# A decoder layer whose second feed-forward stage runs in two passes, with seven block products in place of eight

## The reference, cut to what matters

```python
def layer_norm(x, g, b):
    mu = jnp.mean(x, -1, keepdims=True)
    var = jnp.mean(jnp.square(x - mu), -1, keepdims=True)
    return (x - mu) * lax.rsqrt(var + LN_EPS) * g + b

def swiglu(h, wg, wu, wd):
    return (jax.nn.silu(h @ wg) * (h @ wu)) @ wd

# x: 1024 prompt tokens and 8 sample tokens, D_MODEL = 1024; D_FF = 2816
h = x * (1 + mod[:, 1]) + mod[:, 0]
x = layer_norm(ALPHA * x + 0.5 * mod[:, 2] * swiglu(h, ffn1_wg, ffn1_wu, ffn1_wd), ln_g[0], ln_b[0])
h = x * (1 + mod[:, 4]) + mod[:, 3]
x = layer_norm(ALPHA * x + mod[:, 5] * mixer(h), ln_g[1], ln_b[1])      # ends with mixed @ w_out
h = x * (1 + mod[:, 7]) + mod[:, 6]
x = layer_norm(ALPHA * x + 0.5 * mod[:, 8] * swiglu(h, ffn2_wg, ffn2_wu, ffn2_wd), ln_g[2], ln_b[2])
```

## Time and profile before

| | |
|---|---|
| Runs | 2271.41, 2273.47, 2273.75 us, median 2273.47 |
| Span of the profiled execution, first to last instruction | 2265.1 us (8.4 below the median of the runs; no device time of its own is listed) |
| Mean granted TensorE clock | 0.986 |
| Busy share of the span: TensorE, VectorE, ScalarE, GpSimd | 95%, 34%, 26%, 27% |
| TensorE's share of the chain that ended last | 87% |
| First matmul of the second feed-forward stage | 1459.97 us |
| Last down matmul of it, end | 2220.2 us |
| Mean DMA rate | 76 GB/s |

### The profile page before, as it was taken

The page is one execution under the profiler, slowest core; times in us unless marked ns, Lnnn a source line. Parts: engine busy times, 40 slices in busy tenths (PEclk is TensorE's granted clock), DMA queues, the critical chain, the costliest instruction groups (busy, mean ns, idle before and its releaser), DMA issues.

```text
span 2265.1 us, 33136 instructions
## 1 busy us (share of the span) xinstructions
PE 2161.6 (95%) x13244; PEld 1976.8 (87%) x13244; DVE 778.9 (34%) x1709; ACT 580.7 (26%) x1071; POOL 614.4 (27%) x397
## 2 busy tenths in 40 slices
PE   6799999999999998999979989999999999999997
PEld 2689999999999997998844449899999999999995
DVE  1532122321223229202365652751222211222327
ACT  2311111112111123422265561361111111111114
POOL 1232322223222230124233333132323232323210
PEclk8899999999999999999989999999999999999999
DMA  8372222321321110413242012111111111111002
GB/s 288 131 231 94 84 66 93 112 93 38 112 93 38 47 38 19 148 47 108 101 169 106 1 38 66 38 47 48 56 37 56 37 56 37 56 37 56 28 1 75
DMA packets 168942, 171.36 MB, mean 76 GB/s; under 512 B 14370, under 2 KB 130834, under 8 KB 168324
## 3 DMA queue, kind: packets, MB, share of 16 engines
...
## 4 chain that ended last, share of the span: by engine, by line
PE 87%; DVE 6%; ACT 2%; issue 2%; SPq 2%; DMA 1%; POOL 0%; DVEq 0%; ACTq 0%
PE psum L211 26%; PE psum L213 25%; PE psum L212 25%; PE psum L1086 2%; PE psum L546 2%; PE psum L1145 1%; PE psum L987 1%; DVE NT L694 1%; PE psum L1443 1%; DMA ADA<-in_w_ada 1%; SPq L499 1%; PE psum L644 1%; DVE Y L659 1%; DVE Y L679 1%; PE psum L1136 1%
## 5 line engine op out<-in xcount | busy, mean ns | idle before, releaser
L211 PE MATMUL psum<-Hhi,Whi 128*128 128x344 f32 x2736 | 878.7, 321 | 19.5 <-DVE Hlo L703 10.3
L213 PE MATMUL psum<-Hhi,Wlo 128*128 128x344 f32 x2736 | 875.2, 320 | 0.0
L212 PE MATMUL psum<-Hlo,Whi 128*128 128x344 f32 x2736 | 874.4, 320 | 0.0
L313 POOL TENSOR_TENSOR Wlo<-RAW,Whi 128x1024 fp32r<-128x1024 f32 x158 | 383.2, 2446 | 696.9 <-ACT Whi L309 696.3
L211 PEld LDWEIGHTS psum<-Hhi,Whi 128*128 128x128 f32 x2736 | 515.9, 189 | 29.9 <-issue 23.0
L213 PEld LDWEIGHTS psum<-Hhi,Wlo 128*128 128x128 f32 x2736 | 515.6, 188 | 0.0
L212 PEld LDWEIGHTS psum<-Hlo,Whi 128*128 128x128 f32 x2736 | 514.9, 188 | 0.3
L436 DVE TENSOR_TENSOR GF<-SIL,psum 128x344 f32<-128x344 f32 x132 | 67.6, 512 | 902.7 <-ACT SIL L400 900.1
L443 DVE SCALAR_TENSOR_TENSOR Y<-psum,G,Y 128x344 f32<-128x344 f32 (+1 forms) x528 | 301.2, 573 | 180.5 <-PE psum L213 180.5
L211 PE MATMUL psum<-Ghi,Whi 128*128 128x344 f32 x1056 | 340.2, 322 | 2.4 <-DVE Y L443 2.4
L212 PE MATMUL psum<-Glo,Whi 128*128 128x344 f32 x1056 | 338.0, 320 | 0.0
(11 more groups left out here) (192 smaller groups left out, 1312.0 us busy)
## 6 DMA issues: line engine op xcount, KB each, us to landing
...
RAW<-in_ffn_wg SPq DMA_DIRECT2D x44, 512.0 KB, 3.8
RAW<-in_ffn_wu SPq DMA_DIRECT2D x44, 512.0 KB, 3.7
RAW<-in_ffn_wd SPq DMA_DIRECT2D x44, 512.0 KB, 3.7
...
```

The costliest lines, as they stand in the source:

```text
L211: pe.matmul(out, whi, xhi, start=first, stop=False)
L212: pe.matmul(out, whi, xlo, start=False, stop=False)
L213: return pe.matmul(out, wlo, xhi, start=False, stop=last)
L313: pool.tensor_tensor(Wlo[slot][:, :, :], RAW[raw][:, :, :], Whi[slot][:, :, :].bitcast(F32), ALU.subtract).then_inc(W[phase].ready, 1)
```

## The change

The second feed-forward stage handles the tokens in two passes of 516, each as two sides of `GQ = 258`. In a pass, a chunk takes two tiles of `D_FF` (rows j), two halves of `D_MODEL` (LOWK, HIGHK) and the two sides: a product of 2 by 2 blocks, for the gate and for the up weights. Its eight block products become seven of sums and differences of blocks (`NP = 7`), so 14 products for gate and up, each of 12 matmuls with 258 columns. VectorE forms the sums of weight blocks anew for each chunk and pass (`row_sums`, `row_differences`, 512 elements each), and those of the activations once per pass (`column_sums`, `last_column_sum`). Parts of results shared by several blocks are copied from PSUM by ScalarE (`part_act`) and added by VectorE (`add_dve`). A chunk in a pass then has 16 down units of six matmuls with 258 columns; the down weights are the old ones. All weights are fetched and split once per pass, so twice.

The second norm, the w_out product and the third norm go by four groups of 258. The norm of groups 2 and 3 before the stage runs inside the first pass; the last norm of groups 1 and 0 and the output of their first four blocks of 128 tokens run inside the second pass (`early_turn_pe`, `early_copy_act`, `early_sp`); five blocks are left for after the end. The residual scaling of `Y` goes to GpSimd for groups 0 and 1 (`residual_pool`) and ScalarE for 2 and 3 (`residual_act`).

The core of the diff:

```diff
+GQ = T // 4
+NP = 7
...
+        LOWK, HIGHK = slice(0, KT // 2), slice(KT // 2, KT)
+        W_SOURCE = [[PAIR[u][:, 0, LOWK, :], PAIR[u][:, 0, HIGHK, :], S2[u][:, :, :], S1[u][:, :, :],
+                     PAIR[u][:, 1, LOWK, :], PAIR[u][:, 0, HIGHK, :], PAIR[u][:, 1, HIGHK, :]] for u in range(2)]
...
+        T_SOURCE = [NQ[0][:, LOWK, :], NQ[0][:, HIGHK, :], TS[1][:, :, :], TS[0][:, :, :],
+                    NQ[1][:, LOWK, :], NQ[1][:, HIGHK, :], TS[0][:, :, :]]
...
+        BLOCKS = ((0, 0), (1, 1), (0, 1), (1, 0))
...
+        def pair_fetch(sp, r, f, u, first=False):
+            if not first:
+                sp.wait_ge(r_ready, PR * r + u - 1)
+            for j in range(2):
+                sp.dma_start(PAIR[u][:, j, :, :], pair_source[u][:, :, bass.ds((f + j) * P, P)]).then_inc(pair_in[u], 16)
...
+        def row_sums(dve, r, first=False):
+            for u in range(2):
+                if u == 0 and not first:
+                    dve.wait_ge(r_ready, PR * r - 6)
+                dve.wait_ge(pair_in[u], 32 * r + 32)
+                dve.tensor_tensor(S1[u][:, :, :], PAIR[u][:, 1, LOWK, :], PAIR[u][:, 1, HIGHK, :], ALU.add).then_inc(sums_done, 1)
+            for u in range(2):
+                dve.wait_ge(sums_done, 8 * r + 1 + u)
+                dve.tensor_tensor(S2[u][:, :, :], S1[u][:, :, :], PAIR[u][:, 0, LOWK, :], ALU.subtract).then_inc(sums_done, 1)
+        def row_differences(dve, r):
+            for u in range(2):
+                a21 = PAIR[u][:, 1, LOWK, :]
+                dve.tensor_tensor(a21, PAIR[u][:, 0, LOWK, :], a21, ALU.subtract).then_inc(sums_done, 1)
+            for u in range(2):
+                a12 = PAIR[u][:, 0, HIGHK, :]
+                dve.wait_ge(r_ready, PR * r + 3 + u)
+                dve.wait_ge(sums_done, 8 * r + 3 + u)
+                dve.tensor_tensor(a12, a12, S2[u][:, :, :], ALU.subtract).then_inc(sums_done, 1)
...
+        def column_sums(dve, p):
+            dve.wait_ge(t_src, NP * p + 3)
+            if p:
+                dve.wait_ge(t_ready, NP)
+            dve.tensor_tensor(TS[0][:, :, :], NQ[1][:, LOWK, :], NQ[0][:, LOWK, :], ALU.subtract).then_inc(t_src, 1)
+            dve.wait_ge(t_src, NP * p + 4)
+            dve.tensor_tensor(TS[1][:, :, :], NQ[1][:, HIGHK, :], TS[0][:, :, :], ALU.subtract).then_inc(t_src, 1)
+            b12 = NQ[1][:, LOWK, :]
+            dve.tensor_tensor(b12, NQ[1][:, HIGHK, :], b12, ALU.subtract).then_inc(t_src, 1)
+        def last_column_sum(dve, p):
+            dve.wait_ge(t_ready, NP * p + 4)
+            dve.wait_ge(t_src, NP * p + 5)
+            dve.tensor_tensor(TS[0][:, :, :], NQ[0][:, HIGHK, :], TS[1][:, :, :], ALU.subtract).then_inc(t_src, 1)
...
+        def product_pe(pe, r, n, p, fresh=False, first=False):
+            i, u = n // 2, n % 2
+            a, x = bank[2 * u], bank[2 * u + 1]
+            pe.wait_ge(r_ready, PR * r + n + 1)
+            if fresh and u == 0:
+                pe.wait_ge(t_ready, NP * p + i + 1)
+            if i == 0 and not first:
+                pe.wait_ge((silu_done2, gf_done2)[u], 4 * r)
+            if i == 1 and not first:
+                pe.wait_ge(added[u], 3 * r)
+            if i in (2, 4, 5):
+                pe.wait_ge(part_read, 6 * r + {2: 1, 4: 3, 5: 5}[i] + u)
+            if i in (3, 6):
+                pe.wait_ge(added[u], 3 * r + {3: 1, 6: 2}[i])
+            out = (x if i in (1, 3, 5) else a)[:, 0:GQ]
+            whi, wlo = Rhi[n % NP], Rlo[n % NP]
+            for k in range(KT // 2):
+                pe.matmul(out, whi[:, k, :], Thi[i][:, k, :], start=(k == 0 and i in (0, 1, 3)), stop=False, skip_group_check=True)
+                pe.matmul(out, whi[:, k, :], Tlo[i][:, k, :], start=False, stop=False, skip_group_check=True)
+                last = pe.matmul(out, wlo[:, k, :], Thi[i][:, k, :], start=False, stop=(k == KT // 2 - 1), skip_group_check=True)
+            last.then_inc(prod_done, 1)
+        def down_pe2(pe, r, v, first=False):
+            side, d = 1 - v // KT, v % KT
+            if v == 0:
+                pe.wait_ge(dw_ready, 2 * r + 2)
+            if v % KT == 0:
+                pe.wait_ge(g_ready2, 4 * r + 3 + v // KT)
+            if v >= 3:
+                pe.wait_ge(y_evac2, ROWS2 * r + v - 2)
+            elif not first:
+                pe.wait_ge(y_evac2, ROWS2 * r)
+            bk = bank[4 + v % 3][:, 0:GQ]
+            for j in range(2):
+                last = mm3(pe, bk, Whi[4 + j][:, d, :], Wlo[4 + j][:, d, :],
+                           Ghalf[0][:, j, side, :], Ghalf[1][:, j, side, :], j == 0, j == 1)
+            last.then_inc(down_done2, 1)
...
+        def chunk_act(act, r, first=False, more=True, build=False, std_at=None, square_at=None, early=None):
+            if std_at is not None:
+                std(act, *std_at)
+            part_act(act, r, 0, first)
+            row_hi(act, r, 7, first)
+            part_act(act, r, 1)
+            if first:
+                column_hi(act, 0, 2)
+                column_hi(act, 0, 3)
+            row_hi(act, r, 8, first)
...
+            part_act(act, r, 4)
+            row_hi(act, r, 13, first)
+            part_act(act, r, 5)
+            if build:
+                column_hi(act, 1, 2)
+            for j in range(2):
+                drow_hi(act, r, j, first)
+            if build:
+                column_hi(act, 1, 3)
+            silu_act2(act, r, 1)
+            g_hi_act2(act, r, 1)
+            if build:
+                column_hi(act, 1, 4)
+            silu_act2(act, r, 2)
+            g_hi_act2(act, r, 2)
+            if early is not None:
+                early_copy_act(act, early, 1)
+            if build:
+                column_hi(act, 1, 5)
+            silu_act2(act, r, 3)
+            g_hi_act2(act, r, 3)
...
+        def chunk_pool(pool, r, more=True):
+            for n in range(NP, PR):
+                row_lo(pool, r, n)
+            g_lo_pool2(pool, r, 0)
+            for j in range(2):
+                drow_lo(pool, r, j)
+            for b in range(1, 4):
+                g_lo_pool2(pool, r, b)
+            if more:
+                for n in range(NP):
+                    row_lo(pool, r + 1, n)
...
+        def first_blocks(dve, r):
+            add_dve(dve, r, 0, 0)
+            add_dve(dve, r, 0, 1)
+            gf_dve2(dve, r, 0)
+        def later_blocks(dve, r):
+            add_dve(dve, r, 1, 0)
+            add_dve(dve, r, 1, 1)
+            gf_dve2(dve, r, 1)
+            add_dve(dve, r, 2, 0)
+            add_dve(dve, r, 2, 1)
+            gf_dve2(dve, r, 2)
+            gf_dve2(dve, r, 3)
+        def downs_dve(dve, r, p, more=True, norm=None):
+            for v in range(KT):
+                down_dve2(dve, r, p, v, norm)
+            if more:
+                row_sums(dve, r + 1)
+            elif p:
+                dve.wait_ge(y_evac2, ROWS2 * r + KT)
+                samples_in(dve, ln[3])
+            for v in range(KT, ROWS2):
+                down_dve2(dve, r, p, v, norm)
+        def chunk_dve(dve, r, p, center_at=None, scale_at=None):
+            row_differences(dve, r)
+            if scale_at is not None:
+                scaled(dve, *scale_at)
+            first_blocks(dve, r)
+            if center_at is not None:
+                center(dve, *center_at)
+            later_blocks(dve, r)
+            downs_dve(dve, r, p)
...
+            column_sums(dve, 1)
+            with dve.Fori(5, CH - 1) as c:
+                chunk_dve(dve, c, 0)
+            row_differences(dve, CH - 1)
+            first_blocks(dve, CH - 1)
+            column_lo(dve, 1, 0)
+            column_lo(dve, 1, 1)
+            column_lo(dve, 1, 2)
+            add_dve(dve, CH - 1, 1, 0)
+            add_dve(dve, CH - 1, 1, 1)
+            gf_dve2(dve, CH - 1, 1)
+            column_lo(dve, 1, 3)
+            last_column_sum(dve, 1)
+            add_dve(dve, CH - 1, 2, 0)
+            add_dve(dve, CH - 1, 2, 1)
+            gf_dve2(dve, CH - 1, 2)
+            column_lo(dve, 1, 4)
+            gf_dve2(dve, CH - 1, 3)
+            downs_dve(dve, CH - 1, 0, norm=ln[3])
+            for i in range(5, NP):
+                column_lo(dve, 1, i)
+            dve.wait_ge(res_done, 4)
...
             var_pe(pe, ln[2], 1)
-            ffn_pe(pe, ffn[2], 0, 0, 0, LAST_LATE, fresh=True, late_norm=ln[2])
-            with pe.Fori(1, CH - 1) as c:
-                ffn_pe(pe, ffn[2], c, 6 * c, UNIT_D * c, FULL)
-            ffn_pe(pe, ffn[2], CH - 1, 6 * (CH - 1), UNIT_D * (CH - 1), FULL, norm=ln[3])
+            chunk_pe(pe, 0, 0, fresh=True, first=True, mean=((ln[2], 2), (ln[2], 3)))
+            var_pe(pe, ln[2], 2)
+            chunk_pe(pe, 1, 0)
+            pe.wait_ge(ln_std, ln[2].n_at(2))
+            var_pe(pe, ln[2], 3)
+            with pe.Fori(2, CH) as c:
+                chunk_pe(pe, c, 0)
+            pe.wait_ge(ln_std, ln[2].n_at(3))
+            chunk_pe(pe, CH, 1, fresh=True, mean=((ln[3], 1),))
+            var_pe(pe, ln[3], 1)
```

(87 more changed lines are left out.)

553 lines of the change are left out of this document (374 added, 179 removed).

## The result

The changed kernel takes 2346.62 us (median of 4 runs, 2341.01 to 2349.06), the kernel before beside it 2273.61 (2271.41 to 2280.18): ratio 1.0317, 95% interval 1.0293 to 1.0341. The forecast was 2284, range 2256 to 2322. The profiled execution took 2349.06 us with a span of 2347.3, 82.2 more than the span before; the sum said 10.2 more. The 82 and the 73 differ by which executions were profiled: this one is the longest of its four, and with the same 1.8 us between span and device time the span before stands for 2266.9 us, less than any of its four.

The account below looks back on a forecast made before the run. TensorE, busy 95% of the span, was taken as the bound. Terms -41.9 + 2.7 + 29.4 + 15.8 + 10.7 + 9.5 - 16.0 = +10.2 us on 2273.5 gave 2284 us, range 2256 to 2322.

Parts of the forecast that it names:

- Price of 258 columns: TensorE's 258-column matmul pairs: 258/2.4 plus a fixed 13.9 ns, 121.4 ns each; stage after w_out -41.9 us.
- 117.9: Rival price in ns of a 258-column pair, if the loss is per column: 2262 us, faster; chance 0.22.
- 128.6: Rival price in ns of a 258-column pair, if load and stream share one rate: 2331 us; dearer-pair chance 0.12.
- The formula that the prediction took from the Trainium skill: Matmul start-to-start time of N/2.4 + 2.5 ns: 110.0 for 258 columns, making the sum 75 us lower.
- w_out, +2.7: w_out stage goes from 576 matmuls of 344 columns to 768 of 258, with 192 more loads: +2.7 us.
- Row sums, +29.4: Down 11 waits for a bank behind VectorE's four row sums: 1.4 us, 21 times, +29.4 us.
- Hand-over to the downs at nothing: Entry to the downs in each chunk-pass, through GpSimd's low part: margin 0.7 us, so no cost.
- the split chain late: Rival: low part of block 2 comes 1 to 2 us late every chunk-pass; some +30 us, 2314; chance 0.20.
- Half clock: TensorE at half clock after idling 5 us before its first variance sum, in the start: 2 us allowed.
- The start: From last w_out matmul: first product at 17.9 us, first chunk's downs end at 66.2; 41.8 against 26.0, +15.8 us.
- Last norm and hand-overs: Last norm's work moved inside the stage, +10.7 us, and hand-overs at chunks 1 to 5, 10, 11, 12, 14, +9.5.
- Tail: After the last down, norm and output of the remaining blocks: 29 us against 44.9, -16.0 us.

Follow-up runs that it names:

- bank 7: Silu outputs of blocks 0 to 2 put in PSUM bank 7 instead of SBUF in 19 of 22 chunk-passes, against the changed kernel: 2326.97 us.

## Why the prediction was wrong, step by step

**Price of 258 columns: right.** The 168 product pairs of a settled chunk-pass start 120.0 ns apart on average, and 120.5 is the price in the table, which leaves single short breaks in; 121.4 was forecast, 117.9 and 128.6 were the rivals. Over the stage that is 5 us better than the sum. Why a pair costs some 12.5 ns more than its columns no run tests; the forecast only needed it to stay nearly the same. The formula that the prediction took from the Trainium skill (TensorE: Matmul & The Clock Gate, section Back-to-back issue gap) is given there for an isolated matmul, not for a pair with its load, and its 110.0 ns was not seen.

**w_out, +2.7: right in size.** The 768 pairs took 94.8 to 95.0 us in five of the other twelve traces, as the 92.0 of before and 2.7 say; one of them, with bank 7:

```profile
1351.70:1446.50 94.80, 94.76 (x773) 94.67 (x774) 41.88 (x82) 17.58 (x33) 28.31 (x13) 0.98 0.21 62
```

The profiled execution of the changed kernel had gaps at its start and took 100.6, and the seven others 99 to 101. This differs between the builds for a reason that no run here shows, and was in no term.

**Row sums, +29.4: right in mechanism and place, small in size.** 37.2 us in chunk-passes 1 to 21, where 28.0 of the 29.4 were due: 1.4 in many, 1.9 in the settled ones, 3.4 in one. The first sum is itself held by GpSimd (L1719, mean 830 ns against 684 for a difference of the same size), and the 0.61 us each did not have that.

**Hand-over to the downs at nothing: the step that failed.** The prediction gave a margin of 0.7 us and argued against the rival that "GpSimd's and VectorE's durations now are even". They were not even where both engines read SBUF: the earlier trace rows do not show it, the rows of 1422 us do. The edit made one of two operands move from PSUM to SBUF, so the old multiply's price did not hold beside GpSimd. Priced: 33.9 us of gaps, and part of the 16.4 of slow pairs (bank 7 took 3.7 of them away). Of the gaps 18 us were the held multiply (they go with bank 7), some 10 GpSimd's queue (they go when its splits move, under bank 7), and 6 are left. The rival "the split chain late", 2314 at 0.20, named the place, but put it on every chunk-pass and on load alone; the gap came in 13 of 21.

**Half clock: a term left out.** I allowed 2 us, in the start only. With a gap of 0.8 to 7 us before 13 of 21 first downs and 1.4 to 3.4 before each down 11 but the last, 16.4 us in chunk-passes 1 to 21 and 8.2 in chunk-pass 0 went there. The same 1.9 us before down 11 was followed by half clock in chunk-passes 6 and 8 (35.2 us each) and not in 7, 19 and 20 (33.6); what decides it stays open.

**The start: first product right, the rest short.** First product 20.1 us after w_out (17.9 forecast); chunk-pass 0 ended 81.2 after it (66.2 forecast, and 2 more allowed for half clock). "The rest is fed by ScalarE and GpSimd" was wrong for GpSimd: its residual scaling stood ahead of the row splits. Moving it gave 3 to 4 us by the trace; the rest is VectorE's queue and half clock.

**Last norm and hand-overs: 20.2 us with one variance sum of the norm before, against 26.0 forecast. Tail: 30.5 against 29.** Both within their errors.

The differences add up: chunk-passes 1 to 21 +48.7, the start and chunk-pass 0 +13, w_out +6, where it begins +2.5 (1355.5 against 1353.0), tail +1.5: 71.7, against the 72.0 by which the span missed. So the step that failed is the largest part of the miss and not the whole of it: with the multiply held no more in most chunk-passes (bank 7), the kernel still took 2327.0.
